# Index logits from a stacked high/low query, and one attention head's scores in full float32

## The reference, cut to what matters

```python
SEQ, IDX_HEADS, IDX_DIM, HEAD_DIM, A_HEADS = 512, 16, 64, 128, 8
qi = rope(i_q.reshape(bsz, seq, IDX_HEADS, IDX_DIM), positions)
ki = rope(rms_norm(i_k, g)[:, :, None, :], positions)[:, :, 0, :]
...
logits = jnp.einsum('bqhd,bsd->bqhs', qib, k_idx32) * idx_scale      # 16 index heads, 64 deep
score = jnp.einsum('bqhs,bqh->bqs', jax.nn.relu(logits), wb)          # weighted sum over heads
_, sel = lax.top_k(score, n_sel)                                      # 128 keys are kept
...
s = jnp.einsum('bqhd,bqnhd->bqhn', qb, kg).astype(jnp.float32) * att_scale   # 8 heads, 128 deep
p = jax.nn.softmax(s, axis=-1)
```

## Time and profile before

| | |
|---|---|
| median of three runs | 3493.3 us (3489.96 to 3495.22) |
| the profiled execution, its own time | 3500.6 us |
| its span, first to last instruction | 3498.8 us |
| TensorE matmul busy | 3364.9 us, 96% of the span |
| VectorE, ScalarE, GpSimd busy | 52%, 40%, 12% |
| mean granted TensorE clock | 0.984 of full speed |

### The profile page before, as it was taken

One profiled execution on the slowest core, in us unless ns is written; L12 is line 12 of the kernel. 1 busy time (PEld: TensorE's weight loads), 2 busy tenths in 40 slices (PEclk: granted clock), 3 DMA queues, 4 the chain that ended last, 5 costly groups with the idle time before them and its releaser, 6 DMA issues.

```text
span 3498.8 us, 51676 instructions
## 1 busy us (share of the span) xinstructions
PE 3364.9 (96%) x21012; PEld 2673.5 (76%) x21012; DVE 1818.4 (52%) x2380; ACT 1408.5 (40%) x1616; POOL 415.1 (12%) x718
## 2 busy tenths in 40 slices
PE   7899999999999999999999999999999988999897
PEld 1566888888887788888887867888888866777785
DVE  5745666666667333444423457242424247777445
ACT  1323344344434223444423236141414167777423
POOL 0000222322122000000000000000000023444000
PEclk9999999999999999999999999999999999999898
DMA  9522232333233442222222313333333333332321
GB/s 351 184 73 80 98 102 90 108 102 102 99 104 102 139 145 85 84 84 84 84 90 90 132 62 134 124 122 121 120 120 120 134 93 83 71 88 61 126 97 72
DMA packets 178956, 381.46 MB, mean 109 GB/s; under 512 B 111728, under 2 KB 117104, under 8 KB 145008
## 3 DMA queue, kind: packets, MB, share of 16 engines
q1 hardware_dynamic: 164352, 326.73, 28.3%
q0 software_dynamic: 14448, 52.50, 4.4%
HBM read 342.49 MB, written 35.13 MB: 108 GB/s over the span
## 4 chain that ended last, share of the span: by engine, by line
PE 85%; DVE 4%; DMA 3%; POOLq 3%; SPq 2%; issue 1%; ACT 1%; DVEq 1%; POOL 0%; ACTq 0%
PE PJ L294 18%; PE PJ L296 18%; PE PJ L295 18%; PE AB L294 6%; PE AB L296 6%; PE AB L295 6%; POOLq L1582 1%; POOLq L1579 1%; PE AB L233 1%; DMA WK<-ada 1%; PE AB L681 1%; DMA X<-blocks_scratch 1%; PE AB L1677 1%; PE AB L1686 1%; PE AB L447 1%
## 5 line engine op out<-in xcount | busy, mean ns | idle before, releaser
L294 PE MATMUL PJ<-XH,WH 128*128 128x512 f32 x2848 | 1127.5, 396 | 17.2 <-DVE XL L421 10.3
L296 PE MATMUL PJ<-XH,WL 128*128 128x512 f32 x2848 | 1111.7, 390 | 0.0
L295 PE MATMUL PJ<-XL,WH 128*128 128x512 f32 x2848 | 1110.9, 390 | 0.0
L325 DVE TENSOR_TENSOR WL<-RAW,WH 128x2048 fp32r<-128x2048 f32 (+2 forms) x239 | 543.1, 2273 | 695.3 <-ACT WH L320 691.4
L320 ACT ACTIVATE WH<-RAW 128x2048 fp32r<-128x2048 f32 (+2 forms) x240 | 453.6, 1890 | 914.9 <-PE PJ L296 655.0
L294 PEld LDWEIGHTS PJ<-XH,WH 128*128 128x128 f32 x2848 | 536.2, 188 | 142.4 <-issue 29.7
L296 PEld LDWEIGHTS PJ<-XH,WL 128*128 128x128 f32 x2848 | 535.9, 188 | 113.3
L295 PEld LDWEIGHTS PJ<-XL,WH 128*128 128x128 f32 x2848 | 536.4, 188 | 109.6 <-issue 1.9
L294 PE MATMUL AB<-XH,WH 128*128 128x512 f32 (+1 forms) x960 | 380.9, 397 | 10.0 <-DVE XL L421 7.7
L295 PE MATMUL AB<-XL,WH 128*128 128x512 f32 (+1 forms) x960 | 375.0, 391 | 0.0
L296 PE MATMUL AB<-XH,WL 128*128 128x512 f32 (+1 forms) x960 | 375.0, 391 | 0.0
(11 more groups left out here) (448 smaller groups left out, 3880.5 us busy)
## 6 DMA issues: line engine op xcount, KB each, us to landing
RAW<-w SPq DMA_DIRECT2D x232, 1024.0 KB, 4.9
WK<-ada SPq DMA_DIRECT2D x32, 1024.0 KB, 6.5
GATE<-gate POOLq DMA_DIRECT2D x64, 256.0 KB, 3.1
rkvg_scratch<-WK POOLq DMA_DIRECT2D x16, 1024.0 KB, 4.7
x_scratch<-X POOLq DMA_DIRECT2D x8, 1024.0 KB, 5.9
X<-rkvg_scratch SPq DMA_DIRECT2D x32, 256.0 KB, 3.7
RAW<-rkvg_scratch SPq DMA_DIRECT2D x32, 256.0 KB, 3.5
X<-xT SPq DMA_DIRECT2D x4, 1024.0 KB, 15.8
```

The costliest lines, as they stand in the source:

```text
L294: nc.tensor.matmul(bank[0:width, n, :], hi, xh, start=first, stop=False)
L295: nc.tensor.matmul(bank[0:width, n, :], hi, xl, start=False, stop=False)
L296: m = nc.tensor.matmul(bank[0:width, n, :], lo, xh, start=False, stop=last)
L325: nc.vector.tensor_tensor(WL[k % 2][:, :, 0:w], narrow(RAW[k % 2], w), WH[k % 2][:, :, 0:w].bitcast(F32), ALU.subtract).then_inc(wl_ready, 1)
```

## The change

For the index logits, each head's rotated query is split into a high and a low float32r part, and the two are stacked on 128 partitions: for the head on partitions 0 to 63 the high part stays there and the low part goes to 64 to 127, for the other head the reverse. The stacks of the two heads are in `STACK[0]` (`WK` tiles 4 to 7) and `STACK[1]` (tiles 8 to 11 of `X`). The key, which is on both halves already, is split into `KEY_HI` and `KEY_LO` of 128 partitions. A head's logits are then the stack by `KEY_HI` plus the stack by `KEY_LO`. ScalarE makes the high parts, VectorE the low parts, both in slot 0; two semaphores are renamed for it, and `roped` now counts halves of a unit.

For the last attention head the split of query and key is left out, and its scores are one plain float32 matmul for each block.

```diff
         def att_pe(pe, h, k):
...
             elif k == 2:
+                if is_last(h):
+                    pe.wait_ge(s("at_roped"), 2 * h + 1)
+                    for b in range(TB):
+                        m = nc.tensor.matmul(AB[:, b, 0:ROW_W[b]], wk(4)[:, b * P:(b + 1) * P], wk(5)[:, 0:ROW_W[b]],
+                                             start=True, stop=True)
+                    m.then_inc(s("at_scores"), 1)
+                    return
                 wait(pe, s("at_roped"), 2 * h + 2)
...
             elif k == 2:
-                wait(act, s("at_roped"), 2 * h + 1)
-                nc.scalar.activation(AT_HI, wk(4, 2), ACT.Copy).then_inc(s("at_sd"), 1)
+                if not is_last(h):
+                    wait(act, s("at_roped"), 2 * h + 1)
+                    nc.scalar.activation(AT_HI, wk(4, 2), ACT.Copy).then_inc(s("at_sd"), 1)
...
-                wait(dve, s("at_sd"), 2 * h + 2)
-                nc.vector.tensor_tensor(AT_LO, wk(4, 2), AT_HI.bitcast(F32), ALU.subtract).then_inc(s("at_roped"), 1)
+                if not is_last(h):
+                    wait(dve, s("at_sd"), 2 * h + 2)
+                    nc.vector.tensor_tensor(AT_LO, wk(4, 2), AT_HI.bitcast(F32), ALU.subtract).then_inc(s("at_roped"), 1)
...
+        KEY_HI, KEY_LO = WK_R[:, 10 * SEQ:11 * SEQ], WK_R[:, 11 * SEQ:12 * SEQ]
+        STACK = (WK_R[:, 4 * SEQ:8 * SEQ], X_R[:, 8 * SEQ:12 * SEQ])
+        HALF = [slice(h * IDX_DIM, (h + 1) * IDX_DIM) for h in range(2)]
...
         def qi_logits_pe(pe, u, p):
 
             i, b = p // TB, p % TB
-            wait(pe, ix("roped"), u + 1)
+            wait(pe, ix("qn_lo"), 1 + 2 * u + i // 2 + 1)
             if p >= 2:
                 wait(pe, ix("relu"), LOGIT_PAIRS * u + p - 1)
             for half in range(2):
-                rows = slice(half * IDX_DIM, (half + 1) * IDX_DIM)
-                m = nc.tensor.matmul(AB[:, 2 * (p % 2) + half, 0:ROW_W[b]],
-                                     WK[rows, i * SEQ + b * P:i * SEQ + (b + 1) * P],
-                                     WK[rows, 9 * SEQ:9 * SEQ + ROW_W[b]], start=True, stop=True)
+                z, q = AB[:, 2 * (p % 2) + half, 0:ROW_W[b]], STACK[half][:, i * SEQ + b * P:i * SEQ + (b + 1) * P]
+                nc.tensor.matmul(z, q, KEY_HI[:, 0:ROW_W[b]], start=True, stop=False)
+                m = nc.tensor.matmul(z, q, KEY_LO[:, 0:ROW_W[b]], start=False, stop=True)
             m.then_inc(ix("logits"), 1)
...
         def qi_act(act, u, k):
+            if k == 0:
+                if u == 0:
+                    wait(act, ix("key"), 1)
+                    nc.scalar.activation(KEY_HI, wk(9), ACT.Copy).then_inc(ix("key"), 1)
+                for n in range(2):
+                    at = slice(2 * n * SEQ, 2 * (n + 1) * SEQ)
+                    wait(act, ix("roped"), 2 * u + n + 1)
+                    for h in range(2):
+                        m = nc.scalar.activation(STACK[h][HALF[h], at], WK[HALF[h], at], ACT.Copy)
+                    m.then_inc(ix("sd_hi"), 1)
...
         def qi_dve(dve, u, k):
             if k == 0:
                 wait(dve, ix("swapped"), u + 2)
-                for j in range(4):
-                    nc.vector.tensor_tensor(wk(4 + (j % 4)), AB[:, j, :], SINI, ALU.mult)
-                    nc.vector.tensor_tensor(wk(j), wk(j), COSI, ALU.mult)
-                dve.drain()
-                nc.vector.tensor_tensor(wk(0, 4), wk(0, 4), wk(4, 4), ALU.add).then_inc(ix("roped"), 1)
+                for n in (0, 2):
+                    for j in (n, n + 1):
+                        nc.vector.tensor_tensor(wk(4 + j), AB[:, j, :], SINI, ALU.mult)
+                        nc.vector.tensor_tensor(wk(j), wk(j), COSI, ALU.mult)
+                    dve.drain()
+                    nc.vector.tensor_tensor(wk(n, 2), wk(n, 2), wk(4 + n, 2), ALU.add).then_inc(ix("roped"), 1)
+                if u == 0:
+                    wait(dve, ix("key"), 2)
+                    nc.vector.tensor_tensor(KEY_LO, wk(9), KEY_HI.bitcast(F32), ALU.subtract)
+                for n in range(2):
+                    at = slice(2 * n * SEQ, 2 * (n + 1) * SEQ)
+                    wait(dve, ix("sd_hi"), 1 + 2 * u + n + 1)
+                    for h in range(2):
+                        m = nc.vector.tensor_tensor(STACK[h][HALF[1 - h], at], WK[HALF[h], at],
+                                                    STACK[h][HALF[h], at].bitcast(F32), ALU.subtract)
+                    m.then_inc(ix("qn_lo"), 1)
...
-            pool.wait_ge(ix("roped"), 2)
+            pool.wait_ge(ix("roped"), 4)
```

More of the change, by code:

```diff
@@ L452, in build, with is_last @@
         WK_R = placed("WK_R", [P, NWK * SEQ], WK_AT)
+        X_R = placed("X_R", [P, KT * SEQ], (2 * KT + 4 * SKT) * SEQ)
         AT_HI, AT_LO = WK_R[:, 10 * SEQ:12 * SEQ], WK_R[:, 4 * SEQ:6 * SEQ]
+        def is_last(h):
+            return isinstance(h, int) and h == HEADS - 1
         def att_pe(pe, h, k):
@@ L622, in build @@
         ix = lambda n: s("ix_" + n)
-        for name in ("sq", "stat", "sd", "qn", "swapped", "roped", "key", "logits", "relu", "acc"):
+        for name in ("sq", "stat", "sd_hi", "qn_lo", "swapped", "roped", "key", "logits", "relu", "acc"):
             ix(name)
@@ L631, in kw_pe @@
             elif k == 1:
-                wait(pe, ix("qn"), 1)
+                wait(pe, ix("qn_lo"), 1)
                 nc.tensor.matmul(AB[:, 0, :], mat("swap64"), wk(0), start=True,
@@ L638, in kw_act @@
                 wait(act, ix("stat"), 1)
-                nc.scalar.activation(wk(6), AB[:, 0, :], ACT.Sqrt, bias=SC[:, 0:1]).then_inc(ix("sd"), 1)
+                nc.scalar.activation(wk(6), AB[:, 0, :], ACT.Sqrt, bias=SC[:, 0:1]).then_inc(ix("sd_hi"), 1)
         def kw_act_pre(act):
@@ L648, in kw_dve @@
                 nc.vector.tensor_scalar(wk(17), AB[:, 1, :], WI_SCALE, None, ALU.mult)
-                wait(dve, ix("sd"), 1)
+                wait(dve, ix("sd_hi"), 1)
                 nc.vector.reciprocal(wk(6), wk(6))
@@ L652, in kw_dve @@
                 nc.vector.scalar_tensor_tensor(wk(0), wk(0), col("ikg"), wk(6), ALU.mult,
-                                               ALU.mult).then_inc(ix("qn"), 1)
+                                               ALU.mult).then_inc(ix("qn_lo"), 1)
             elif k == 1:
```

## The result

The changed kernel ran in 3477.44 us (median of five, 3471.64 to 3479.95), the kernel before beside it in 3489.96 (3489.59 to 3495.22). The ratio on record is 0.9945, 95% interval 0.9933 to 0.9958: faster by 19 us of 3490, where 15.4 were forecast. The median lies half a microsecond from the forecast time, which is luck with runs that spread over 8 us; by the ratio on the base of that session the time is 3490 x 0.9945 = 3471 us, just under the range's lower end. The ratio is an estimate with an error of its own: the quotient of the means of the times listed is 0.9955 (15.8 us), that of the medians 0.9964. So the question behind the result is whether there is a gain beyond 15.4 us, and where it comes from.

What follows compares the result with a forecast made beforehand. TensorE was taken to bound the kernel, busy for 96%; 10.2 us at the logits plus 5.2 at the last head make 15.4, from the median 3493.3 to 3477.9 us, range 3472 to 3486.

Steps and rivals of the forecast that it cites:

- The logits: TensorE's 32 logit pairs: four pairs cost 2.55 us instead of 3.82, a gain of 10.2 us.
- the fixed cost of the half-height form: Logit pairs before: 0.41 us on top of the stream, believed to belong to the 64-partition form; nearly all the gain.
- B: Logits: fixed cost comes with any break in the weight stream and stays; program gains 2.2 us, 3491; chance 0.06.
- D: Logits: each change of stack and bank costs TensorE a gap; at 0.41 us, 10.8 us slower, 3504; chance 0.03.
- The stacks: Slot 0: VectorE completes the first pair's stacks at 213.9, TensorE wants them at 214.24; no wait.
- rival A: Stacks come late, by up to 1.8 and 1.1 us in units 0 and 1; 6 us lost, 3484; chance 0.12.
- The ring: Relu and additions on ScalarE and VectorE: 1.94 us per pair against TensorE's 2.0, just fast enough; TensorE does not wait.
- The last head: TensorE's wait ahead of the scores goes, 15.59 us become 10.35; gain 5.2 us, worst case 4.2.
- clock part: Last head: some 1.6 us of the 5.2, as without idle time the clock has no reason to fall.
- Later stages follow TensorE's progress, so I expect the shift to reach the end: Everything after the edited places: the whole 15.4 us gain was expected to reach the program's end.
- The range: Program time: 3472 to 3486 us, covering the forecast, C and A, leaving out B, D, E and a tail.

Runs made afterwards that it cites:

- e4: Changed kernel with each head's logits as one 64-partition float32r matmul, low parts left out; profile only, period 7.75 us, 2.28 for four pairs.
- e5: Changed kernel with every low subtraction that fills the stacks made twice, each behind a VectorE drain; profile only, 8.5 us lost over both units.
- e3: Kernel before with only the last head's plain float32 scores put in, logits as before; ratio 0.9980 (0.9971 to 0.9990).
- e6: Changed kernel with the last head's split and TensorE's wait for it kept, scores plain float32; profile only, 5.7 us lost at the last head.
- e2: Changed kernel with the last attention head as before, so the stacked logits alone; ratio 0.9961 (0.9948 to 0.9975).
- e1: Changed kernel run once more with no edit; ratio 0.9937 (0.9924 to 0.9950).
- e7: Changed kernel with plain float32 scores and no query and key split in all eight heads; profile only, together 0.6 us lost.
- e8: Changed kernel with plain float32 scores in the last two heads, last attention group peeled from TensorE's loop; ratio 0.9955 (0.9941 to 0.9968).
- e0: Kernel before, unchanged, against itself; ratio 0.9999 (0.9990 to 1.0009).

## Why the prediction was right, and where it was wrong

**The logits.** Forecast 10.2 us, measured 10.0. The prices of head 0's scores carried over: 8.07 us for a period against 8.02. That the gain is the fixed cost of the half-height form was an inference from one place where matmuls begin without a gap; e4 showed it, with 0.43 us in float32r. Rivals B and D fell already with the changed kernel's rows, where no gap stands ahead of a pair or inside it. The streams alone would have lost: 2.15 us for four pairs before, 2.55 now. The Trainium skill, TensorEngine Tiling, "When to Use Tiling", advises two-fold row tiling for a contraction of 64. The traces agree that the two halves overlap, and show 0.4 us of fixed cost beside it, of which that section has nothing.

**The stacks.** TensorE's matmuls did not wait, as forecast, but with nothing in hand where 0.3 us were reckoned: VectorE's chain from the first multiplication to the stacks took 10.55 us (202.63 to 213.18) instead of 10.46, TensorE came 0.1 us sooner because the pairs before had a gap ahead of them (213.92 to 214.24, a pitch of 0.32), and the weight load waited 0.16. In unit 0 the forecast held by luck of the last tenth of a microsecond. The bound for rival A, 6 us for stacks 1.8 and 1.1 us late, fits e5: stacks 2.8 and 1.9 us late cost 8.5.

**The ring.** It keeps up: VectorE is what ended 12.8 of the 18.4 us of ScalarE's waiting, and TensorE did not wait.

**The last head.** Forecast 5.2, measured 5.2 (e3: 5.3). e6 shows that the wait and the clock behind it are all of it. (The six matmuls "of 0.63 us each" of the prediction are four, one of 0.60 and one of 0.41; they fill the same 2.38 us.) Its clock part is not as firm as I had put it: e2 had nearly the same wait at another time and lost nothing by the clock, so with the logits' shift alone the old code was 2.2 us cheaper here. The two edits' gains therefore don't simply add at this place: alone they are 12.2 us (logits and last head together) and 5.3, together 15.2. Nor is the float32 form shown to be the only remedy. The low part takes 1.22 us; TensorE waited 3.62 because the weights' low part (line 325, 2.28 us) stands ahead of it on VectorE. Made in that one's place, from 1142.54 on, it would have ended near 1143.8 and left a wait of some 1.5 us (an estimate from the earlier trace rows). That order was not run.

**The step that failed** is "Later stages follow TensorE's progress, so I expect the shift to reach the end": it puts every stretch that the edits don't touch at nothing, and makes the sum 15.4 us. Between 326 and 2800 us it is off by 0.6 us in one stretch, of which 0.3 are the first profile's own, and it fails in another. At the layer norm the same code, later or earlier by a few us, passes with one or with two stretches at the lower clock level, and the changed kernel gains 1.5 us there. It did so in the profiles of the changed kernel, e1, e2, e3, e4 and e7, and not in e5, e6 and e8, nor in any of the kernel before. The sum up to 2800 us is then 17.3 us (e1: 17.5), a ratio of 0.9950. By the means of the listed times the changed kernel gained 15.8 us in its first session and 18.5 in e1, with 17.3 between them. By the ratios 0.9945 and 0.9937 two to five microseconds remain; they lie within the intervals (0.9950 is the upper end of the second), and the recurrence stage, which spreads over 15 us by itself, is large enough for them. Whether any part of them is a real effect stays open.

**The range** was built from prices of the edits alone and set on a base of 3493.3 us. The base moves: the same kernel gave medians of 3493.3, 3489.96 and 3495.2. With 17.3 us in place of 15.4 and a base of 3490 the time is 3472.7, at the range's end; the ratio's 3471 is beyond it. The spread of the runs shown, 3490 to 3495 with a profiled execution of 3500.6, told this ahead of time and should have been taken in.

## What to carry to other kernels

A pair of half-height matmuls put into a stream of full-height ones cost 0.4 us beside its stream here, so a form that fills the full height won even with a slightly longer stream; ask what the neighbours in the stream are before tiling the array. Where TensorE waits for the making of high and low parts, plain float32 can be the faster form, and where it does not wait it cost 0.24 us more for 1280 columns; look first whether the part could be made sooner. A gain of half a percent must be read from the places that changed, against a null run: here a stage that nobody touched moved by 15 us.

## What was not expected of the hardware

Whether the granted clock falls behind a short idle time of TensorE is not told by its length alone: it fell behind 3.62, 3.80 and 3.98 us (kernel before, e6, e0), but also behind 2.37 and 1.86 (kernel before, e5), and did not behind 3.10 and 2.80 (e2, e5). So moving unchanged code in time gave or took 1.1 to 1.5 us at the layer norm and 2.2 at the last head, of which 0.5 are the shorter wait.
